# Next map's scores moved behind the transposes of the probabilities in single-map attention jobs of a hybrid encoder step

## The reference, cut to what matters

```python
h = rms_norm(x, g_mix)
(aq, ak, av, bq, bk, bv, ccq, cckv, ckr, dq, dk, dv, dfl) = jnp.split(h @ w_in, offs, axis=-1)
# A (window, sinks, ALiBi), C (latent), D (forgetting): one softmax map for each head
s = einsum(q, k) * scale + bias          # then masked
m = s.max(axis=-1); p = exp(s - m); p = p / p.sum(axis=-1)
o = einsum(p, v)
# B (differential): two maps for each head, w = a[0] - lam * a[1], then one product with v
x = x + concatenate([oa, ob, oc, od]) @ w_out
x = x + square(relu(rms_norm(x, g_mlp) @ w_up)) @ w_down
x = x + (ple @ w_ple) * sigmoid(rms_norm(x, g_ple) @ w_ple_gate)
```

## Time and profile before

| | us |
|---|---|
| median of three runs | 3640.94 |
| the execution that was profiled | 3643.79 |
| its span in the profile | 3642.0 |
| TensorE (PE) matmul busy in it | 3403.4 (93%) |
| VectorE (DVE) busy | 1429.3 (39%) |
| ScalarE (ACT) busy | 1124.0 (31%) |
| GpSimd (POOL) busy | 1900.3 (52%) |

### The profile page before, as it was taken

One profiled execution on the slowest core, in us unless ns is written; L12 is line 12 of the kernel. 1 busy time (PEld: TensorE's weight loads), 2 busy tenths in 40 slices (PEclk: granted clock), 3 DMA queues, 4 the chain that ended last, 5 costly groups with the idle time before them and its releaser, 6 DMA issues.

```text
span 3642.0 us, 58666 instructions
## 1 busy us (share of the span) xinstructions
PE 3403.4 (93%) x20676; PEld 3061.5 (84%) x20676; DVE 1429.3 (39%) x2287; ACT 1124.0 (31%) x1614; POOL 1900.3 (52%) x1189
## 2 busy tenths in 40 slices
PE   7998988899999999999979998888999999999988
PEld 5776755599999999998967776556999999999988
DVE  5334544474042240425362344344830513304263
ACT  2333322233333333332333332222333333333322
POOL 4554200077667676677565551001776676766764
PEclk9999988899999999999989999889999999999999
DMA  5333412144444444444343333122444444444433
GB/s 164 102 112 104 119 51 73 46 150 151 145 145 153 143 151 151 139 153 143 117 133 107 113 93 111 54 71 74 140 152 142 149 152 140 151 141 148 151 121 122
DMA packets 295722, 453.09 MB, mean 124 GB/s; under 512 B 36336, under 2 KB 111344, under 8 KB 294832
## 3 DMA queue, kind: packets, MB, share of 16 engines
q1 hardware_dynamic: 295328, 448.66, 39.0%
q0 software_dynamic: 144, 0.87, 0.1%
HBM read 435.54 MB, written 14.06 MB: 123 GB/s over the span
## 4 chain that ended last, share of the span: by engine, by line
PE 83%; DVE 8%; issue 4%; ACT 2%; DMA 1%; SPq 1%; POOL 0%; DVEq 0%; ACTq 0%; POOLq 0%
PE ps L687 19%; PE ps L686 19%; PE ps L685 18%; PE ps L783 4%; PE ps L746 4%; PE ps L749 4%; PE ps L771 4%; PE ps L748 3%; PE ps L852 1%; DMA ring<-in_w_in 1%; DVE ssq L1346 1%; PE ps L821 1%; ACT prob L1115 1%; PE ps L887 1%; PE ps L856 1%
## 5 line engine op out<-in xcount | busy, mean ns | idle before, releaser
L649 POOL TENSOR_TENSOR wlo<-ring,whi 128x1024 fp32r<-128x1024 f32 x600 | 1479.7, 2468 | 1310.8 <-ACT whi L1100 1310.8
L1100 ACT ACTIVATE whi<-ring 128x1024 fp32r<-128x1024 f32 x600 | 635.1, 1060 | 1418.7 <-PE ps L687 1414.5
L685 PE MATMUL ps<-xhi,wlo 128*128 128x320 f32 x2560 | 802.5, 313 | 23.9 <-issue 13.5
L686 PE MATMUL ps<-xlo,whi 128*128 128x320 f32 x2560 | 797.6, 312 | 0.0
L687 PE MATMUL ps<-xhi,whi 128*128 128x320 f32 x2560 | 797.0, 311 | 0.0
L687 PE MATMUL ps<-hhi,whi 128*128 128x320 f32 x2176 | 673.1, 309 | 0.0
L685 PE MATMUL ps<-hhi,wlo 128*128 128x320 f32 x2176 | 660.9, 304 | 0.0
L686 PE MATMUL ps<-hlo,whi 128*128 128x320 f32 x2048 | 629.9, 308 | 0.0
L636 POOL TENSOR_TENSOR rlo<-ring,whi 128x256 fp32r<-128x256 f32 (+2 forms) x576 | 416.8, 758 | 387.2 <-ACT whi L1084 387.0
L685 PEld LDWEIGHTS ps<-xhi,wlo 128*128 128x128 f32 x2560 | 486.5, 190 | 29.3 <-issue 27.6
L686 PEld LDWEIGHTS ps<-xlo,whi 128*128 128x128 f32 x2560 | 486.6, 190 | 1.0 <-issue 0.4
(11 more groups left out here) (240 smaller groups left out, 3284.5 us busy)
## 6 DMA issues: line engine op xcount, KB each, us to landing
ring<-in_w_up SPq DMA_DIRECT2D x256, 512.0 KB, 3.6
ring<-in_w_down SPq DMA_DIRECT2D x256, 512.0 KB, 3.5
ring<-in_w_in SPq DMA_DIRECT2D x120, 512.0 KB, 3.5
ring<-in_w_out SPq DMA_DIRECT2D x64, 512.0 KB, 3.9
ring<-in_w_ple_gate SPq DMA_DIRECT2D x64, 512.0 KB, 3.5
xsave<-x SPq DMA_DIRECT2D x8, 640.0 KB, 7.3
x<-xsave SPq DMA_DIRECT2D x8, 640.0 KB, 4.9
ring<-in_w_in SPq DMA_DIRECT2D x16, 288.0 KB, 2.8
```

The costliest lines, as they stand in the source:

```text
L649: nc.gpsimd.tensor_tensor(wlo[:, s, :], ring[:, s, :], whi[:, s, :].bitcast(f32), ALU.subtract)\
L685: mm(out, lo[:, k, cols], xh, start=start, stop=False)
L686: mm(out, hi[:, k, cols], xl, start=False, stop=False)
L1100: A(whi[:, s, :], ring[:, s, :], ACT.Copy).then_inc(hi_ready, 1)
```

## The change

In items of A, C and D the scores of the following map come behind the transposes on TensorE, its exponentials behind the copy of the sample part on ScalarE, and its bias and maxima behind the copy of the prompt part and `filled` of T on VectorE. Group B keeps its order. No instruction is added or taken away.

```diff
@@ TensorE, attention
                     fill(l, j, f"S{i}")
-                    for m in following[0:1]:
-                        score_map(l, j * MAPS + m)
+                    if g == "B":
+                        for m in following[0:1]:
+                            score_map(l, j * MAPS + m)
                     fill(l, j, f"T{i}")
                     transpose_probs(l, it)
+                    if g != "B":
+                        for m in following:
+                            score_map(l, j * MAPS + m)
                     fill(l, j, f"V{i}")
                     hold(probT_copied[0], l * N_ITEMS + it + 1)
                     hold(probT_copied[1], l * N_ITEMS + it + 1)
-                    for m in following[1:2]:
-                        score_map(l, j * MAPS + m)
+                    if g == "B":
+                        for m in following[1:2]:
+                            score_map(l, j * MAPS + m)
                     weigh_values(l, it)
@@ ScalarE, attention
-                    exps(l, j, it + 1, following[0:1])
+                    if GROUPS[j] == "B":
+                        exps(l, j, it + 1, following[0:1])
                     halves(l, HALVES.get((j, f"T{i}"), ()))
...
                         .then_inc(probT_copied[0], 1)
+                    if GROUPS[j] != "B":
+                        exps(l, j, it + 1, following)
                     halves(l, HALVES.get((j, f"V{i}"), ()))
-                    exps(l, j, it + 1, following[1:2])
+                    if GROUPS[j] == "B":
+                        exps(l, j, it + 1, following[1:2])
@@ VectorE, attention
                     filled(l, j, f"S{i}")
-                    bias_and_max(l, j, following[0:1])
+                    if g == "B":
+                        bias_and_max(l, j, following[0:1])
...
                     filled(l, j, f"T{i}")
-                    bias_and_max(l, j, following[1:2])
+                    bias_and_max(l, j, following[1:2] if g == "B" else following)
                     dve.wait_ge(out_ready, l * N_ITEMS + it + 1)
```

## The result

The changed kernel takes 3609.7 us (median of 4 runs, 3603.5 to 3612.88) against 3642.35 us for the kernel before (4 runs, 3637.8 to 3648.24): a ratio of 0.9911, 95% interval 0.9894 to 0.9928, or 33 us less. The profiled executions have spans of 3642.0 and 3607.4 us, 34.6 us apart. The forecast was 3628 with a range from 3612 to 3643: right in direction, too small by 18 us.

A forecast was written before the change was run, and what follows sets the result against it. TensorE was taken to bound the kernel (83% of the chain). Waits gained 14.6 - 10.7 + 1.0 = 4.9 us a layer, 10 in two: 3640.9 to 3631; clock 3 more: 3628 us, range 3612 to 3643.

The forecast's parts named there:

- The waits taken away: Jobs 4 to 7: 12 of 16 TensorE waits for `probT` copies go, saving 14.6 us in each layer.
- The waits added: Ahead of transposes in jobs 4 to 7, up to 2.29 us at first ones, 0.74 later; 10.7 us a layer.
- the rival of longer hand-offs: From exponentials to transposes, 0.3 us more at the 12 waits of a layer, so 3635 us; chance 0.20.
- The sum at full clock: Waits in jobs 0, 1 and 4 to 7: 4.9 us gained a layer, 10 in two, giving 3631.
- the two chunk copies: In jobs 0 and 1, TensorE waits longer for them: 1.3 us lost in job 1, 1.1 in job 0.
- The clock: TensorE's granted clock in jobs 4 to 7: a small gain of 3 us, from 3631 to 3628.
- The bound of 28 us for the one-block jobs: Jobs 4 and 6 of both layers: all time lost to the clock regained, 28 us at most.
- The rival of a clock granted more freely: With less idle time everywhere, half of the one-block jobs' 28 us comes back, so 3617 us; chance 0.17.
- The slower rival: First transposes of jobs 4 and 6: the new 2.2 us wait takes the clock down, 3656 us; chance 0.10.
- Its companion: Transposes of jobs 4 and 6: transpose mode never engages full clock, so wait and transposes make 3 us below it.

The follow-up runs named there:

- the V1 edit: Changed kernel with job 1's V1 piece moved to T1; run only with other edits: first items in old order 3579.0 us, throwaway matmuls 3564.8 us.

## Why the prediction was wrong

**The waits taken away: right.** 12 of 16 waits for `probT` went from each layer's jobs 4 to 7, the fourth items' stayed at 0.97.

**The waits added: right, a little too high.** First transposes waited 2.00 and 2.13 us in the first layer, 2.01 and 2.30 in the second (worked out: 2.17 and 2.29, of which a row shows 0.16 less, since it counts from the modelled end of the matmul). Later ones waited 0.27 in C and 0.40 in D, with that overlap 0.43 and 0.56, where 0.62 and 0.74 were worked out; the products take a little longer in the new order (1.58 for 1.55) and the scores ahead of them too (1.97 for 1.87). The round of job 4 is 7.08 us, worked out 7.1. From the end of the scores to the transposes it is 4.23 us (487.33 to 491.56), worked out 4.33, so the rival of longer hand-offs, with 0.3 us more, is out.

**The sum at full clock: somewhat low.** For jobs 4 to 7 it was 3.9 us in a layer. The following are estimates from the runs above. With half clock out of the way the old order takes about 280 us in both layers (the old order with throwaway matmuls, less their overrun) and the new one 267 (the new one with them, 267.6), 6.4 in a layer: jobs 5 and 7 gave 2.5 and 2.4 (worked out 2.3 each), jobs 4 and 6 some 0.8 each instead of nothing. In jobs 0 and 1 the two chunk copies did what was said, 3.55 us of wait in job 1 (3.6) and 1.04 in job 0 (1.1). The profile puts the 1.04 down to GpSimd's `rlo`, which ended at 139.06; the chunk copy ended at 138.75, and TensorE went on at 139.18, so either could have been the last and the two are not told apart. In jobs 0 and 1 the waits' net was 1.3 us for both layers, worked out 2. Together 14 us of waits for the 10 of the sum.

**The clock: the step that failed.** "I take a small gain, 3 us, since total idle time falls". Measured: jobs 4 to 7 lost about 26 us to it before (305.7 less 280) and 10 after (276.8 less 267), so 16 us came back there; in jobs 0 and 1, for which no clock term stood in the sum at all, 5 us in the two profiled executions and about 10 on average over those above. The bound of 28 us for the one-block jobs was too wide: they had lost about 20 (152.6 less 132), since half clock there costs 0.4 us of time a microsecond and not 0.5, and the two-block jobs about 5, which was not in it. Of this the one-block jobs got back 11 and the two-block jobs all 5. The rival of a clock granted more freely, with a chance of 0.17 and a price of 3617, was the nearer one. Three things in the working led astray. Idle time was weighed by its total, which changes little in jobs 4 and 6, while the run with throwaway matmuls shows that the 1.0 to 1.7 us of standing still in each round cost 26 us of clock. The jobs that had full clock where the prediction looked were booked as having nothing to gain, though elsewhere they did not have it: job 7 had none in the first layer, but 10 us of half clock in the second. And the 0.95 of job 5 in the earlier trace rows is not job 5's: the row runs to 606, and half clock sets in at 602.0 and goes on into the next stage; the job itself, 565.3 to 603.1, was at 0.99.

**The slower rival** said that the new first wait takes the clock down. For job 6 this holds: it keeps 12.7 us of half clock, 10.2 of them from 640.8, right behind the wait at 639.53, and they go when the wait goes or is filled. In job 4 a wait of the same length did no such thing in either layer of the changed kernel, but did in one execution with C and D alone. So its mechanism is real and its size was smaller than what the other removed waits gave. Its companion, that transposes keep the clock down, gets no support: in the old order with throwaway matmuls all eight jobs ran at 1.00 with their transposes in.

What stays open: why job 6 loses its clock after a first wait of 2.1 us and job 4 mostly keeps it after 2.0. The two differ in what comes before (the forget gates' small matmuls against latents) and this was not separated. In jobs 0 and 1 the clock's gain is measured, but no run ties it to a gap: the order takes away 3.2 us of waits in a layer and adds 2.4. Nor was the V1 edit run without the others, though job 1, where it acts, gave 5.5 and 5.1 us with it.

## What to carry to other kernels

Price a wait on TensorE twice: by its length, and by the clock that the work behind it then runs at; here the second was the larger, 21 us against 14. Read the granted clock by stage, over more than one execution if there are more: job 7 of the second layer was at 0.88 in the profile of the kernel before and at 1.00 in that of group A alone, with the same order in it. To find out what a wait costs, put throwaway matmuls into it: if the time falls, the clock was being lost, and the order of the work is worth changing or the gap worth filling.

## What the runs showed that was not expected

A kernel became 22 us faster by 96 more matmuls in gaps of 1.0 to 1.7 us, and the changed kernel 45 us faster (3609.7 to 3564.8) with 120 of them in waits that stayed and one fill piece moved. Replacing a wait of 2.1 us by one of 1 us took 6.5 us off a stage 37 us long. A wait of 3.55 us in a stage of 73.8 us, brought down to 1.06, took 5.5 us off the stage.
